# Reordering VectorE's work inside the seven-product turns of three feed-forward stages

## The reference

```python
def conv_ffn(h, w_up, conv_w, conv_b, w_down):
    L = h.shape[1]
    u = h @ w_up                                   # 1024 -> 2 x 2816
    up = jnp.pad(u, ((0, 0), (CONV_WIDTH - 1, 0), (0, 0)))
    u = conv_b + sum(conv_w[j] * up[:, j:j + L] for j in range(CONV_WIDTH))   # 3 taps over positions
    gate, val = jnp.split(u, 2, axis=-1)
    return (jax.nn.silu(gate) * val) @ w_down      # 2816 -> 1024
```

## Time and profile before

| | |
|---|---|
| median of 3 runs | 2001.38 us (1997.85 to 2002.08) |
| profiled execution | 2004.72 us, of which the span of its instructions 2002.9 us |
| TensorE busy | 1928.4 us |
| VectorE, ScalarE, GpSimd busy | 1232.9, 975.0, 973.5 us |
| mean granted TensorE clock | 0.986 |

### The profile page before, as it was taken

One profiled execution on the slowest core, in us unless ns is written; L12 is line 12 of the kernel. 1 busy time (PEld: TensorE's weight loads), 2 busy tenths in 40 slices (PEclk: granted clock), 3 DMA queues, 4 the chain that ended last, 5 costly groups with the idle time before them and its releaser, 6 DMA issues. The chain is left out here.

```text
span 2002.9 us, 35610 instructions
## 1 busy us (share of the span) xinstructions
PE 1928.4 (96%) x13702; PEld 1780.4 (89%) x13706; DVE 1232.9 (62%) x1896; ACT 975.0 (49%) x1650; POOL 973.5 (49%) x570
## 2 busy tenths in 40 slices
PE   8999999999999999999999998999999998999997
PEld 6888888889889988999777998999899898999897
DVE  6964540227878782166676377898722767888702
ACT  3333433333666662256676444655524444656432
POOL 2536424442576654425555347655542246655442
PEclk9999999999999999999999999999999999999999
DMA  8932002221457743312100225764322125765321
GB/s 337 340 135 94 17 7 94 96 96 51 113 141 188 185 132 104 108 64 96 43 1 1 85 72 126 172 169 127 116 86 84 43 77 125 169 169 132 114 93 54
DMA packets 129893, 222.99 MB, mean 111 GB/s; under 512 B 8144, under 2 KB 97488, under 8 KB 129744
## 3 DMA queue, kind: packets, MB, share of 16 engines
q1 hardware_dynamic: 102560, 193.55, 28.7%
q0 software_dynamic: 25344, 25.17, 8.3%
q10 hardware_dynamic: 1840, 2.19, 0.3%
HBM read 218.78 MB, written 2.10 MB: 110 GB/s over the span
## 5 line engine op out<-in xcount | busy, mean ns | idle before, releaser
L1988 POOL TENSOR_TENSOR w_lo<-w_raw,w_hi 128x1024 fp32r<-128x1024 f32 x167 | 416.9, 2501 | 529.9 <-ACT w_hi L2246 504.0
L2246 ACT ACTIVATE w_hi<-w_raw 128x1024 fp32r<-128x1024 f32 (+2 forms) x299 | 290.3, 981 | 480.7 <-PE PS L1022 392.9
L2131 POOL TENSOR_TENSOR w_lo<-w_raw,w_hi 128x1024 fp32r<-128x1024 f32 x96 | 272.6, 2959 | 167.0 <-ACT w_hi L2246 167.0
L1022 PE MATMUL PS<-mid_hi,w_lo 128*128 128x256 f32 (+2 forms) x968 | 230.9, 296 | 9.8 <-DVE work L3574 8.9
L1847 PE MATMUL PS<-D_hi,w_lo 128*128 128x256 f32 (+2 forms) x768 | 220.5, 287 | 16.2 <-DVE c L3678 16.2
L1022 PE MATMUL PS<-mid_hi,w_hi 128*128 128x256 f32 (+2 forms) x968 | 228.4, 294 | 0.0
L1022 PE MATMUL PS<-mid_lo,w_hi 128*128 128x256 f32 (+2 forms) x968 | 228.4, 294 | 0.0
L1847 PE MATMUL PS<-D_lo,w_hi 128*128 128x256 f32 (+2 forms) x768 | 220.3, 287 | 0.0
L1847 PE MATMUL PS<-D_hi,w_hi 128*128 128x256 f32 (+2 forms) x768 | 220.1, 287 | 0.0
L1022 PE MATMUL PS<-H_hi,w_lo 128*128 128x512 f32 (+3 forms) x672 | 204.4, 339 | 0.3 <-DVE H_lo L3160 0.3
L1022 PE MATMUL PS<-H_lo,w_hi 128*128 128x512 f32 (+3 forms) x672 | 203.4, 337 | 0.0
(11 more groups left out here) (463 smaller groups left out, 4686.4 us busy)
## 6 DMA issues: line engine op xcount, KB each, us to landing
w_raw<-stream SPq DMA_DIRECT2D x289, 512.0 KB, 3.5
ada_w<-ada SPq DMA_DIRECT2D x48, 512.0 KB, 6.9
w_raw<-stream POOLq DMA_DIRECT2D x24, 512.0 KB, 9.6
w_s<-stream SPq DMA_DIRECT2D x12, 512.0 KB, 5.5
w_s<-stream POOLq DMA_DIRECT2D x12, 512.0 KB, 7.2
w_s_odd<-stream SPq DMA_DIRECT2D x12, 512.0 KB, 5.4
w_s_odd<-stream POOLq DMA_DIRECT2D x12, 512.0 KB, 6.1
X<-xT SPq DMA_DIRECT2D x8, 256.0 KB, 5.9
```

Source lines behind the costliest of these rows:

```text
L1022: last = pe.matmul(out[:, c0 + a:c0 + b], w, x[:, a:b], start=start and i == 0, stop=stop and i == 2)
L1988: gp.tensor_tensor(w_lo[:, o], w_raw[:, o], w_hi[:, o].bitcast(F32), ALU.subtract)\
L2131: gp.tensor_tensor(t.part(w_lo, q), t.src(f, p), t.part(w_hi, q).bitcast(F32), ALU.subtract)\
L2246: return act_.activation(out, in_, ACT.Copy, scale=scale)
```

## The change

Four edits, on GpSimd, ScalarE and VectorE. TensorE's and SyncE's orders stay.

1. In front of the seven-product turns: VectorE makes sum2(0) between D7 and D6, and does the taps of classic turn 2 before low part 2, its gated products behind it. ScalarE rounds product 2's weights before, and the four D operands between and behind its four last taps.
2. GpSimd makes D4's low part behind product 4's low part.
3. In each turn VectorE puts the two joins of product 4 ahead of the gated products, and the joins of product 5 ahead of sum2 (in the last turn: ahead of the first two `lower_mid`).
4. Behind the last turn of up_b and up_c, the late taps go tile by tile (`taps_by_tile`) and ahead of `lower_mid(2)` and `(3)`, and ScalarE's `round_mid(4)`, `(5)` go behind its taps.

```diff
@@ GpSimd, lower_turns
-                for d in range(4):
+                for d in range(3):
                     lower_operand(t, d)
                 for f in range(FAST):
                     ...
                     fast_lower(t, f, 4)
+                    if f == 0:
+                        lower_operand(t, 3)
                     fast_lower(t, f, 6)
@@ ScalarE, ffn
-                for p in range(2):
+                for p in range(3):
                     fast_upper(t, 0, p)
-                for d, (hi, x) in enumerate(((D6_hi, D6), (D5_hi, D5), (D7_hi, D7), (D4_hi, D4))):
-                    act_.wait_ge(df_ok, D_0 + 2 * t.l + (2 if d == 3 else 1))
-                    copy(hi[:, 0:4 * t.n], x[:, 0:4 * t.n]).then_inc(dh_ok, 1)
-                fast_upper(t, 0, 2)
-                take(2, psum)
+                for m in range(4):
+                    wait_tile(act_, up, 0, m, 2)
+                    wait_work(t, 2, m)
+                    last_tap(t, 2, m, lambda a, b: psum(m)[:, a:b], t.a, t.T).then_inc(y_ok, 1)
+                    if m < 2:
+                        round_operand(t, m)
+                round_operand(t, 2)
+                round_operand(t, 3)
+                for j in range(2):
+                    gate_silu(t, 2, j)
...
-                round_mid(t, 4)
-                round_mid(t, 5)
+                if t.l == 0:
+                    round_mid(t, 4)
+                    round_mid(t, 5)
                 fast_tap(t, FAST - 1, 2)
                 fast_tap(t, FAST - 1, 3)
+                if t.l:
+                    round_mid(t, 4)
+                    round_mid(t, 5)
@@ VectorE, ffn
+                def taps_by_tile(f):
+
+                    g, cut_ = CLASSIC + f, t.t0 + t.n
+                    for m in (2, 3):
+                        wait_first_tap(g, m)
+                        chain.done(tap_of(g, m, 0, t.u22(m), cut_, t.T))
+                        chain.done(tap_of(g, m, 0, t.u(f, m), max(t.a, 1), cut_))
+                        chain.wait()
+                        chain.done(tap_of(g, m, 1, t.u22(m), cut_, t.T))
+                        tap_of(g, m, 1, t.u(f, m), max(t.a, 2), cut_).then_inc(free[m], 1)
...
                     chain.done(v.tensor_tensor(d7, b22, b12, ALU.subtract))
+                    sum2(0)
                     chain.wait()
...
                 operands()
-                sum2(0)
+                taps(2, 0, lambda m: lambda a, b: psum(m)[:, a:b])
+                taps(2, 1, lambda m: lambda a, b: psum(m)[:, a:b])
                 fast_lower(0, 2)
-                body(2, psum)
+                gated(2, 0)
+                gated(2, 1)
                 signs()
...
                     fast_lower(f, 5)
+                    join(f, 4, 0)
+                    join(f, 4, 1)
                     if f:
                         gated(g - 1, 0)
                         gated(g - 1, 1)
+                    join(f, 5, 0)
+                    join(f, 5, 1)
                     if f + 1 < FAST:
                         sum2(f + 1)
                     else:
                         lower_mid(0)
                         lower_mid(1)
-                    join(f, 4, 0)
-                    join(f, 4, 1)
-                    join(f, 5, 0)
-                    join(f, 5, 1)
                     taps(g, 0, lambda m: t.u(f, m))
+                if t.l:
+                    taps_by_tile(FAST - 1)
                 lower_mid(2)
                 lower_mid(3)
-                late_taps(FAST - 1)
+                if t.l == 0:
+                    late_taps(FAST - 1)
```

More of the change, by code:

```diff
@@ L2615, in round_mid, with round_operand @@
                 copy(ht(mid_hi, k, t.T)[:, t.a:], ht(mid_f, k, t.T)[:, t.a:]).then_inc(midh_ok, 1)
+            def round_operand(t, d):
+                hi, x = ((D6_hi, D6), (D5_hi, D5), (D7_hi, D7), (D4_hi, D4))[d]
+                act_.wait_ge(df_ok, D_0 + 2 * t.l + (2 if d == 3 else 1))
+                copy(hi[:, 0:4 * t.n], x[:, 0:4 * t.n]).then_inc(dh_ok, 1)
             def ffn(t, psum0, psum, behind_first=None, behind_up=None):
@@ L3676, in join @@
                             t.wait_operands(v, 2)
+                        if f and t.l:
+                            chain.wait()
                         t.wait_kept(v, f, 5 + c)
```

## The result

The changed kernel takes 2050.02 us (median of 4 runs, 2047.68 to 2055.03), the kernel before 2001.73 beside it (4 runs, 1997.85 to 2007.05): ratio 1.024, 95% interval 1.021 to 1.027. I had forecast 2020, range 1974 to 2042: slower as forecast, by two and a half times the amount. The profiled execution took 2047.68 us, span 2045.9 (2004.72 and 2002.9 before).

What follows compares the result with a forecast made beforehand. TensorE, busy 96% of the span, was taken to bound the kernel, losing time to waits for VectorE. First turns -13.8, middles +38.9 and tails -6 made +19.1 us, so 2020 us as a median; range 1974 to 2042.

Steps and rivals of the forecast that it cites:

- What bounds, and the hold: TensorE bounds, 96% busy; in mid-turn, two GpSimd subtractions behind a DMA issue hold a waiting VectorE operation, 6.05 us.
- First turn: Start of each up stage: taps ahead of low parts cut 19.8 us of loss to 6, gaining 13.8.
- my own condition for the long hold: GpSimd's bursts in the turns: behind a DMA issue two GpSimd operations run without letting waiting VectorE in.
- My own sign for it: First turn: that part is wrong if PE waits over 4 us between products 1 and 3.
- GpSimd's edit: D4's low part behind low part 4: costs nothing, as no product needs D4 before product 6, 11 us later.
- Middle: Turns 1 to 7: join waits go, but VectorE always meets GpSimd's burst, 24.3 us per turn; +38.9 us net.
- Tail: Behind up_b and up_c: taps by tile free PE's bank earlier, 3 us gain in each stage, 6 together.
- The first (each boundary hands over): Turns: GpSimd lets VectorE in at each boundary, or VectorE keeps its hold; mid waits vanish; 1957 us; chance 0.16.
- The second: Turns: the loop closes only in part, 0.8 us shorter and not at all in up_a; 1985 to 1998; chance 0.15.
- The third, half clock every turn: Turns: waits of 3.9 us bring half clock each time, 25.0 us a turn; 2031, up to 2042; chance 0.15.

Runs made afterwards that it cites:

- pool_short: Changed kernel, but in the turns behind the first GpSimd's low parts of products 0 and 1 subtract only 64 of 1024 columns; 1979.27 us, ratio 0.990.
- dma_last: Changed kernel with GpSimd's add DMA for product 4's block issued behind its low parts of products 0 and 1, not ahead of both; 2006.89 us, ratio 1.004.
- mid_back: Changed kernel with VectorE's order inside the turns as before, first turn and tail as changed; 1997.32 us, ratio 1.000.
- both_short: Changed kernel with GpSimd's low parts of products 0 and 1 (turns 1 to 7) and 4 (turn 0) cut to 64 of 1024 columns; 1963.9 us, ratio 0.983.
- d4_back: Changed kernel with GpSimd's D4 low part back in front of product 4's low part; 2047.81 us, ratio 1.025.
- tail_only: Kernel before with only the change's last part, the late taps by tile and the later round_mid; 1993.05 us, ratio 0.997.
- start_dma: Changed kernel, but in turn 0 GpSimd issues the add for turn 1 behind low part 4 and D4's low part; 2043.76 us, ratio 1.022.

## Why the forecast had the sign and not the size

**What bounds, and the hold.** Right in kind. pool_short takes the subtractions away and every middle wait goes with them; dma_last shows that the DMA issue ahead makes the hold long. How long was wrong: two operations there, but in mid_back as many as GpSimd had in the row, five.

**First turn: the step that failed.** "I count 2 us residual per stage (between 0 and 4)", a gain of 13.8; the profile has a loss of 5.2, so 19.0 of the 23.9 us between forecast span difference (19.1) and measured one (43.0). Product 0 does start on time. I had named what is late next, VectorE's low parts 2 and 3, but priced it against GpSimd's D subtractions at 2.4 us each, and not against GpSimd's next sequence: add, low part 4, D4's low part, which begins with a DMA issue, my own condition for the long hold. In the kernel before, GpSimd issued that add at 1232.93, computed low part 4 only from 1236.53, behind a wait for ScalarE, and had done D4's low part already, while sum4 took 1.22 us. In the changed kernel everything is ready when the load lands late, so the three come in one row, and a VectorE operation falls into it in each stage. both_short shows it: with low part 4 short the loss is 5.2, near the 6 that I forecast, and the change is worth -16.5. My own sign for it came true: PE waits over 4 us between products 1 and 3 of the first turn in up_a and up_c (4.66 and 4.91), and at product 4 in up_b (4.46). I also costed GpSimd's edit at nothing. d4_back puts its place at 3.4 us in the first turns and 2 in the whole, and D4's low part is one of the two that hold. A smaller slip, of no weight in the sum: the wait of 3.70 us in up_a stands before product 1, not before the stage's first product (PE's first product there begins at 557.57).

**Middle.** Right: +39.8 against +38.9. VectorE's first taps in up_b stand 24.65 and 24.11 us apart (1271.74, 1296.39, 1320.50) where I had 24.3. up_a lost 14.4 (I had 13.3), up_b 24.9 and up_c 25.7 (25.1 each). Inside that turn low part 6 starts 12.8 us behind the first tap (I had 13.0), and product 4's second join ends 14.7 behind it (14.4). Two things in it are not as I wrote. The first gated product is the one that stands in 8 of the 12 turns 1 to 6 of up_b and up_c, and the second gets through; either way the pair ends with the burst. And the weight sum that grows is sum4, 3.4 us in six turns of each of the two stages, held by low part 4; sum2, which I had named, stays at 1.21. The leg still comes to 12.8 us, since the late taps, of which one stood 2.59 us in the turn that my 13.0 is from, run free there: that part of the agreement is luck. In up_a PE's six waits (0.87 to 1.91 us) end with ScalarE's kept sum; the low part of product 2 that I had named is done at the same moment (1.22 us from 633.41, PE starts at 634.68).

**Tail.** -2.0 instead of -6: -3.8 in up_b and up_c, and 1.8 lost behind up_a, where VectorE's last turn has the new order too and I had no term. By itself the edit is worth about 6 (tail_only). In the changed kernel PE waits 3.91 and 3.70 us for the taps at down; in mid_back, with the same tail but the old turn order, 4.7 us in two waits. So the turn order gives part of it back, in the way I described and had priced too low. That it does so even without the long hold is read from both_short, where 7.5 us in two waits are left.

**Scale.** The medians differ by 48.3 us, the spans by 43.0: the profiled executions lie 2.3 below and 3.0 above their medians.

**Rivals.** The first (each boundary hands over) describes what dma_last does, not what the changed kernel does: of the three ways the middle could go, only the long hold fits. The second did not occur. The third, half clock every turn, is not needed: the clock over the middles is 0.95 to 0.97, and the turns of up_b and up_c stay at 24.5 us on average.

**The rule of the Trainium skill.** In dma_last and start_dma a waiting VectorE instruction got in at the end of the running subtraction. The Trainium skill, page "SBUF — State Buffer", section "Who interferes with whom", says that whoever issues first gets the shared pair for the whole instruction; these two traces agree. Those of the changed kernel and of mid_back don't: with a DMA issue ahead, one instruction stood for two subtractions (6.69 us) and for five (13.17 us).

**Open.** That the issue matters is shown; why is not. The traces show one thing that goes with it. Between two full-length subtractions in a row that follows a DMA issue without a gap, the second is on record 0.12 to 0.84 us before the first has ended (1253.23 and 1255.60 above: 0.53); without an issue ahead it is 0.01 to 0.08 (1249.74 and 1252.54 in start_dma: 0.03). Over all sixteen traces VectorE operations with all their operands in SBUF stood at 204 such boundaries: they got in at all 98 without an issue ahead and at none of the 106 with one. So the hold in mid_back ran over five subtractions because GpSimd's row had five: sum4 came through ahead of it, ScalarE rounded in time, and nothing made GpSimd stop. Why the records overlap behind an issue, and why the short low part in both_short lets sum4 in, stays open.

## What to carry to other kernels

Before moving a VectorE operation with SBUF operands, write down what GpSimd runs at its new time, over the whole stage and not only in the steady turns, and price the meeting at the length of GpSimd's whole row when a DMA issue leads it. Where GpSimd must both issue a DMA and compute, issue behind the arithmetic: that one line was worth 43 us here, but only in the order in which VectorE met the row. Time each hunk of a change by itself: the tail's hunk gains about 6 us alone and is hidden inside a change that loses 48.

## What the runs showed of the hardware

A VectorE operation of 48 columns, 0.18 us long, stood for 5.80 us, and one of 1.22 us for 13.17 us, beside GpSimd subtractions that followed a GpSimd DMA issue. Without the issue ahead the same subtractions let VectorE in at each boundary: 2.38, 2.90 and 2.20 us for one operation. I had taken the longest hold to be two subtractions, 6.05 us.
